# Attention sink as a column of the scores, weights normalised on ScalarE, and three steps moved in VectorE's order

## The reference, cut to what matters

```python
def swa_sink_attention(q, k, v, sinks):
    ...
    s = jnp.einsum("bnqhgd,bnkhd->bnhgqk", qb, kb, ...) * (HEAD_DIM ** -0.5)
    ...
    s = jnp.where(mask[None, :, None, None], s, NEG)
    sk = sinks.astype(jnp.float32).reshape(N_KV_HEADS, GROUP)[:, :, None, None]
    m = jnp.maximum(jnp.max(s, axis=-1, keepdims=True), sk)
    e = jnp.exp(s - m)
    p = e / (jnp.sum(e, axis=-1, keepdims=True) + jnp.exp(sk - m))
    o = jnp.einsum("bnhgqk,bnkhd->bnqhgd", p.astype(v.dtype), vb)
```

## Time and profile before

| what | value |
|---|---|
| median of 3 runs | 2660.0 us (2658.65 to 2663.03) |
| the profiled execution | 2658.19 us, of which the span 2656.4 us |
| TensorE matmuls busy | 2619.3 us (99%) |
| VectorE busy | 1601.4 us (60%) |
| ScalarE busy | 1028.5 us (39%) |
| GpSimd busy | 410.3 us (15%) |
| mean granted clock of TensorE | 0.998 of full speed |
| 762 to 854 us (first half of the beats) | TensorE 82.1, VectorE 84.1, ScalarE 58.1 of 92 us |
| 854 to 942 us (second half) | TensorE 87.8, VectorE 80.3, ScalarE 61.3 of 88 us |

### The profile page before, as it was taken

One profiled execution on the slowest core, in us unless ns is written; L12 is line 12 of the kernel. 1 busy time (PEld: TensorE's weight loads), 2 busy tenths in 40 slices (PEclk: granted clock), 3 DMA queues, 4 the chain that ended last, 5 costly groups with the idle time before them and its releaser, 6 DMA issues.

```text
span 2656.4 us, 33800 instructions
## 1 busy us (share of the span) xinstructions
PE 2619.3 (99%) x12616; PEld 2116.1 (80%) x12616; DVE 1601.4 (60%) x2440; ACT 1028.5 (39%) x1334; POOL 410.3 (15%) x147
## 2 busy tenths in 40 slices
PE   8999999999999999999999999999999999999998
PEld 6767888888876778888888888888888888888886
DVE  4467211213999976579998988888344444444444
ACT  4465322214346763232223455555332222222223
POOL 0001455542010003424444000000000000000000
PEclk9999999999999999999999999999999999999999
DMA  5111222222222222223333365465565555555552
GB/s 184 48 48 69 97 102 97 99 95 95 95 84 76 68 80 96 95 95 145 148 142 143 135 230 192 186 233 201 198 229 189 189 189 191 195 197 195 194 196 95
DMA packets 121737, 374.37 MB, mean 141 GB/s; under 512 B 7553, under 2 KB 73217, under 8 KB 92737
## 3 DMA queue, kind: packets, MB, share of 16 engines
q1 hardware_dynamic: 117968, 333.74, 35.5%
q10 hardware_dynamic: 2016, 35.26, 3.4%
q0 software_dynamic: 1680, 4.46, 0.6%
HBM read 301.86 MB, written 69.21 MB: 140 GB/s over the span
## 4 chain that ended last, share of the span: by engine, by line
PE 83%; DVE 13%; issue 2%; ACT 2%; DMA 0%; DVEq 0%; POOL 0%; POOLq 0%; ACTq 0%
PE ps L1042 26%; PE ps L1044 25%; PE ps L1043 25%; PE ps L1552 2%; DVE cand_t L2179 1%; DVE z L1910 1%; DVE cand_t L2175 1%; DVE sel L2181 1%; DVE wl L1640 1%; DVE topi L2141 1%; DVE topi L2151 1%; DVE sc L2144 1%; DVE sel L2184 1%; DVE bpos L2141 1%; DVE bpos L2151 1%
## 5 line engine op out<-in xcount | busy, mean ns | idle before, releaser
L1042 PE MATMUL ps<-hh,wh 128*128 128x512 f32 x1968 | 783.3, 398 | 9.3 <-DVE wl L1646 8.0
L1044 PE MATMUL ps<-hh,wl 128*128 128x512 f32 x1968 | 768.8, 391 | 0.0
L1043 PE MATMUL ps<-hl,wh 128*128 128x512 f32 x1968 | 767.8, 390 | 0.0
L531 ACT ACTIVATE wh<-raw 128x2048 fp32r<-128x2048 f32 x217 | 414.9, 1912 | 771.2 <-PE ps L1044 769.9
L2208 DVE TENSOR_TENSOR wl<-raw,wh 128x2048 fp32r<-128x2048 f32 x101 | 231.3, 2290 | 432.8 <-ACT wh L531 432.8
L1042 PEld LDWEIGHTS ps<-hh,wh 128*128 128x128 f32 x1968 | 370.2, 188 | 98.9 <-issue 15.6
L1044 PEld LDWEIGHTS ps<-hh,wl 128*128 128x128 f32 x1968 | 370.0, 188 | 79.3
L1043 PEld LDWEIGHTS ps<-hl,wh 128*128 128x128 f32 x1968 | 370.7, 188 | 74.3 <-issue 1.0
L1042 PE MATMUL ps<-gah,wh 128*128 128x512 f32 x1024 | 398.7, 389 | 0.0
L1044 PE MATMUL ps<-gah,wl 128*128 128x512 f32 x1024 | 398.7, 389 | 0.0
L1043 PE MATMUL ps<-gal,wh 128*128 128x512 f32 x1024 | 398.7, 389 | 0.0
(11 more groups left out here) (259 smaller groups left out, 3006.8 us busy)
## 6 DMA issues: line engine op xcount, KB each, us to landing
raw<-in_w_slots SPq DMA_DIRECT2D x217, 1024.0 KB, 4.8
a_spill<-ast SPq DMA_DIRECT2D x64, 512.0 KB, 2.6
gate_table<-stage ACTq DMA_DIRECT2D x8, 4096.0 KB, 13.0
at<-a_spill SPq DMA_DIRECT2D x64, 512.0 KB, 5.8
tt<-gate_table SPq DMA_DIRECT2D x64, 512.0 KB, 6.8
lnb<-z POOLq DMA_DIRECT2D x36, 64.0 KB, 1.9
xT<-in_x SPq DMA_DIRECT2D x4, 512.0 KB, 7.2
bt<-in_rel_tiles POOLq DMA_DIRECT2D x1, 2048.0 KB, 12.2
```

The lines of the kernel that those rows point to most:

```text
L531: act.activation(wh[:, b, :], raw[:, b, :], ACT.Copy).then_inc(sem("w_hi"), 1)
L1042: nc.tensor.matmul(bank, whi, xhi, start=start, stop=False)
L1043: nc.tensor.matmul(bank, whi, xlo, start=False, stop=False)
L1044: return nc.tensor.matmul(bank, wlo, xhi, start=False, stop=stop)
```

## The change

- The buffer `tmp` gets four more columns. Seen by the attention (`spr`), it is now two steps of two heads of 257 columns: the last is the sink's.
- GpSimd writes -sink into that column (`sink_column`), for every step, between the swaps in its queue. It waits until the Exp of two steps earlier is done.
- ScalarE's `exps` takes exp over the scores and the sink's column at once, so that the accumulated sum is already the denominator. The two activations for exp(sink - m) go.
- The reciprocal moves to ScalarE: Ln of the sum, then Exp of minus that, each waiting for the one before on its own engine. `scaled(n)` now follows `exps(n)` in the same beat.
- VectorE's `shares` goes. Its tap moves to the end of the beat.
- In VectorE's order the low part at t = 6 goes ahead of the five taps of that tile (those of t = 8, 10, ... stay behind theirs). The rotation of K2 goes from t = 20, behind taps and low part, to t = 19, ahead of the seven taps; that of Q2 stays at t = 21 but goes ahead of the taps.
- Behind the beats VectorE does 12 taps instead of 2 before the last `y_low`.

```diff
--- before.py
+++ after.py
@@ -210,7 +210,8 @@
         def esb(name, shape, dt=F32, stack=None):
             return (stack or early).enter_context(nc.sbuf_tensor(name, shape, dt))
 
-        tmp = esb("tmp", [P, 2, S])
+        tmp_all = esb("tmp_all", [P, 2 * S + 4])
+        tmp = tmp_all[:, 0:2 * S].rearrange("p (a n) -> p a n", a=2)
         sqb = esb("sqb", [P, 2, S])
         lnb = esb("lnb", [P, 2, S])
 
@@ -251,7 +252,8 @@
         nsink = esb("nsink", [P, 2 * SWA_PAIRS], stack=two)
         kdup = esb("kdup", [P, 2, S], stack=two)
 
-        spr, spt = (x.rearrange("p r (e n) -> p r e n", e=2) for x in (tmp[:, :, :], sqb[:, :, :]))
+        spr = tmp_all[:, :].rearrange("p (r e n) -> p r e n", r=2, e=2)
+        spt = sqb[:, :, :].rearrange("p r (e n) -> p r e n", e=2)
         swapped = lnb[:, 0, :]
 
         two.close()
@@ -497,9 +499,23 @@
                     of = to + HD // 2 if to % HD == 0 else to - HD // 2
                     pool.dma_start(swapped[to:to + HD // 2, :], u_tile(tile)[of:of + HD // 2, :]).then_inc(sem("swap_in"), 16)
 
+            def sink_column(n):
+
+                p = n // NT
+                if n == 0:
+                    pool.wait_ge(sem("rp_s"), 1)
+                if n >= 2:
+                    pool.wait_ge(sem("sw_e"), 2 * n - 2)
+                pool.tensor_copy(spr[:, n % 2, :, 2 * P:2 * P + 1],
+                                 nsink[:, 2 * p:2 * p + 2].rearrange("p (e n) -> p e n", n=1)).then_inc(sem("sw_k"), 1)
+
             swap_halves(K2, 0)
-            for p in range(SWA_PAIRS):
-                swap_halves(Q2 + p, p + 1)
+            swap_halves(Q2, 1)
+            swap_halves(Q2 + 1, 2)
+            for n in range(SWA_STEPS):
+                sink_column(n)
+                if n % NT == 2 and n // NT + 2 < SWA_PAIRS:
+                    swap_halves(Q2 + n // NT + 2, n // NT + 3)
 
             pool.wait_ge(sem("w_lo"), FIRST["co"] + 2 + 2)
             lows(FIRST["co"] + 2, FIRST["out2"] + 2)
@@ -783,19 +799,21 @@
 
                 c, st, p = swa_cols(n), sstat[:, n % 2, :], n // NT
                 act.wait_ge(sem("sw_m"), 2 * n + 2)
+                act.wait_ge(sem("sw_k"), n + 1)
                 for e in range(2):
-                    act.activation(spr[:, n % 2, e, c:], spr[:, n % 2, e, c:], ACT.Exp, bias=st[:, 2 + e:3 + e], scale=-1.0,
-                                   accum_out=st[:, 6 + e:7 + e]).then_inc(sem("sw_e"), 1)
-                for e in range(2):
-                    act.activation(st[:, 8 + e:9 + e], st[:, 2 + e:3 + e], ACT.Exp, bias=v("sinks", 2 * p + e)
-                                   ).then_inc(sem("sw_e"), 1)
+                    act.activation(spr[:, n % 2, e, c:2 * P + 1], spr[:, n % 2, e, c:2 * P + 1], ACT.Exp,
+                                   bias=st[:, 2 + e:3 + e], scale=-1.0, accum_out=st[:, 6 + e:7 + e]).then_inc(sem("sw_e"), 1)
 
             def scaled(n):
 
                 c, st = swa_cols(n), sstat[:, n % 2, :]
+                act.wait_ge(sem("sw_e"), 2 * n + 2)
+                act.activation(st[:, 8:10], st[:, 6:8], ACT.Ln).then_inc(sem("sw_a"), 1)
+                act.wait_ge(sem("sw_a"), n + 1)
+                act.activation(st[:, 12:14], st[:, 8:10], ACT.Exp, scale=-1.0).then_inc(sem("sw_r"), 1)
                 act.wait_ge(sem("sw_r"), n + 1)
                 for e in range(2):
-                    act.activation(spr[:, n % 2, e, c:], spr[:, n % 2, e, c:], ACT.Copy, scale=st[:, 12 + e:13 + e]
+                    act.activation(spr[:, n % 2, e, c:2 * P], spr[:, n % 2, e, c:2 * P], ACT.Copy, scale=st[:, 12 + e:13 + e]
                                    ).then_inc(sem("sw_p"), 1)
 
             def turned_weights(n):
@@ -822,12 +840,11 @@
             def beat(n):
                 if n >= 7 and (n - 7) % NT == 0:
                     heads_out((n - 7) // NT)
-                if 0 <= n - 1 < SWA_STEPS:
-                    scaled(n - 1)
                 if 0 <= n - 2 < SWA_STEPS:
                     turned_weights(n - 2)
                 if n < SWA_STEPS:
                     exps(n)
+                    scaled(n)
 
             def in2_out(t):
 
@@ -1968,20 +1985,11 @@
                 if n >= 2:
                     dve.wait_ge(sem("sw_t"), n - 1)
                 for e in range(2):
-                    dve.tensor_tensor_reduce(spr[:, n % 2, e, c:], ps[:, 3 + e, c:2 * P], msk[:, c:], -SCALE,
+                    dve.tensor_tensor_reduce(spr[:, n % 2, e, c:2 * P], ps[:, 3 + e, c:2 * P], msk[:, c:], -SCALE,
                                              nsink[:, 2 * p + e:2 * p + e + 1], ALU.add, ALU.min,
                                              accum_out=st[:, 2 + e:3 + e]).then_inc(sem("sw_m"), 1)
                 taps(1)
 
-            def shares(n):
-
-                st = sstat[:, n % 2, :]
-                dve.wait_ge(sem("sw_e"), 4 * n + 4)
-                dve.tensor_tensor(st[:, 10:12], st[:, 6:8], st[:, 8:10], ALU.add).then_inc(sem("sw_a"), 1)
-                taps(1)
-                dve.wait_ge(sem("sw_a"), n + 1)
-                dve.reciprocal(st[:, 12:14], st[:, 10:12]).then_inc(sem("sw_r"), 1)
-
             def y_low(p):
 
                 dve.wait_ge(sem("at_h"), p + 1)
@@ -1989,15 +1997,13 @@
 
             def beat(n):
                 taps(1)
-                if 0 <= n - 1 < SWA_STEPS:
-                    shares(n - 1)
                 if n < SWA_STEPS:
                     masked(n)
                 if n % NT == 1 and n // NT + 1 < SWA_PAIRS:
                     roped(Q2 + n // NT + 1, n // NT + 2, "sw_q")
                 if n >= 9 and (n - 9) % NT == 0:
                     y_low((n - 9) // NT)
-                taps(1)
+                taps(2)
 
             g0 = FIRST["in2"]
             dve.wait_ge(sem("ns"), 1)
@@ -2009,16 +2015,18 @@
                     beat(n)
                 if t <= RAW_TILES:
                     scaled_out(t - 1)
-                if RAW_TILES <= t < BEAT_TILE0:
-                    taps(7 if t % 2 else 5)
-                if t % 2 == 0 and t < Z2_TILES:
+                if t % 2 == 0 and t <= RAW_TILES:
                     weight_low(g0 + t // 2 + 1)
                 if t == 4:
                     scaled_x()
-                if ORDER2[t - 1] == Q2 + 1:
+                if ORDER2[t - 1] == Q2:
                     roped(K2, 0, "rk")
                 if ORDER2[t - 1] == Q2 + 2:
                     roped(Q2, 1, "sw_q")
+                if RAW_TILES <= t < BEAT_TILE0:
+                    taps(7 if t % 2 else 5)
+                if t % 2 == 0 and RAW_TILES < t < Z2_TILES:
+                    weight_low(g0 + t // 2 + 1)
                 if t == 30:
                     ln_sums(0)
                     ln_sums(1)
@@ -2034,7 +2042,7 @@
                 dve.tensor_tensor(u_tile(GATTN + n), u_tile(GATTN + n), ps[:, AO_BANKS[n], :], ALU.mult
                                   ).then_inc(sem("ev_ao"), 1)
 
-            taps(2)
+            taps(12)
             y_low(SWA_PAIRS - 1)
             weight_low(g0 + 1)
             taps(KD * conv_steps)
```

## The result

The changed kernel takes 2683.2 us (median of 6 runs, 2682.3 to 2683.7) beside 2659.9 us for the kernel before on the same chip (6 runs, 2658.3 to 2663.0): ratio 1.0088, 95% interval 1.0078 to 1.0097. That is outside the range that I gave, on the other side of no change.

The account below looks back on a forecast made before the run. TensorE's queue, busy 2619.3 of 2656.4 us, was taken as the bound. Opening +1.1, later waits -6.2, half speed -1.9 and +1.0 gave -6.0: 2652.2 for the profiled execution, 2654.0 us as median, range 2649.5 to 2660.

Parts of the forecast that it names:

- The rest: Outside the main terms: one more column in two Exps under 0.01 us; the 16-byte longer buffer shifting others, nothing.
- the likeliest case: The forecast itself, 2654.0 us for the whole kernel, given chance 0.48 and a range between 2651.5 and 2657.
- my two signs of being wrong: Attention stage: step-2 masking ending before 777 us, or taps beside the column copies lasting longer than 0.75 us.
- The rival for the slower side: Ln and Exp each load a table in every beat, or shifted buffers cost something: 2686 us, chance 0.07.
- The chain from Ln to the scaling: ScalarE, each beat: dependent Ln and Exp cost 0.65 us, 0.2 more than the removed activations, 6 us in all.
- The opening (+1.1): Attention's start: moved low part and rotations leave VectorE idle 2.1 us, and TensorE passes step 2's masking 1.1 us later.
- The next low parts have more room than that: Opening, VectorE: running 2.1 us later does no harm; the low part at 752.71 serves a tile nine microseconds later.
- Half speed in the opening (+1.0): Near 775 us: a 3.5 us TensorE wait brings a 1.9 us half-speed stretch, half vanishing in the next ScalarE wait.
- The waits behind it (-6.2): After the opening: TensorE's waits for maskings, ScalarE's copies and layer-norm sums fall from 8.5 to 2.3 us.
- the end (-1.9): Attention's tail: the half-speed stretch at 961.87, behind the 2.85 us wait at 961.22, disappears, saving 1.9 us.
- 64 steps of 0.08 us: VectorE's shares: removing thirty-two pairs of small operations, each stepping by 0.08 us, frees 4.9 us of its time.
- GpSimd's copies: Attention beats: sink-column copies and VectorE taps exclude each other, adding 3.2 to 12.8 us on VectorE; 2655.3 to 2659.1, chance 0.17.

Follow-up runs that it names:

- e5_still: Kernel after, with the four extra columns overlapping a buffer idle in the attention stage, so nothing behind moves: 2652.1 us, 0.997 of the kernel before.
- e2_shift: Kernel before with only an unused 32-byte buffer per partition ahead of the shared buffer `tmp`, shifting all behind it by 32 bytes: 2689.2 us, ratio 1.0107.
- e6_low_back: e5_still with the low part of tile 6 put back behind its five taps, rotations still ahead: 2651.1 us beside 2652.1.
- s1_sweep: Kernel before with only the gather's streamed buffers padded to distances of 128, 192, 256 and 512 bytes from the weights', modulo 2048: 2673.5 us, one run.
- e8_best: e5_still with three of tile 6's taps ahead of the low part, two taps instead of seven before the first masking, five moved to later beats: 2648.0 us, 0.9954.

## Why the prediction was wrong, by its own steps

**The rest: "I know no cost, and matmuls last 0.39 whether they stream from one buffer or another, so nothing".** This is the step that failed. I had seen that the buffer grows by 16 bytes and moves all behind it. My reason for pricing that at nothing was a row of durations in a layout in which all these buffers lay a multiple of 2048 bytes from the weights: it could not show what another distance does, and a duration rounded to 0.01 us hides 6.7 ns. The term is +31.0 us (after against e5_still), +29.5 alone (e2_shift). Without it the forecast would have been near: e5_still is 7.8 us under before, where the sum said 6.0, inside the likeliest case's range. Neither of my two signs of being wrong came up (the step-2 masking ends at 779 us in e5_still, the taps stay at 0.73 us): both watched only the stage that was changed.

**The rival for the slower side** named "any cost of the shifted buffers" but priced a table load. That its 2686 us lie near the measured 2683.2 is luck, for no table load comes in the beats (the first behind 764 us is one of 1.28 us at 949.51, behind them). Ln and Exp, on ScalarE in the kernel after:

```profile
777.01 0.20 ACT L811 ACTIVATE sstat<-sstat 128x2 f32<-128x2 f32 x1
777.25 0.20 ACT L813 ACTIVATE sstat<-sstat 128x2 f32<-128x2 f32 x1
777.48 0.91 ACT L816 ACTIVATE tmp_all<-tmp_all,sstat 128x256 f32<-128x256 f32 x2
```

The chain from Ln to the scaling is 0.47 us, not 0.65: equal to the two activations that went. I had taken the duration of the activations of one column with a bias per partition (L790), 284 ns; these, of two columns and without one, last 204 (mean of 32 each), and start 0.24 us apart.

**The opening (+1.1).** In e5_still the first low part starts at 682.60, VectorE idle for 2.00 us ahead, as described. The next starts at 695.50, and TensorE waits for it:

```profile
682.60 2.29 DVE L1658 TENSOR_TENSOR wl<-raw,wh 128x2048 fp32r<-128x2048 f32 x1 [2.00 <-ACT wh L548]
...
695.50 2.28 DVE L1658 TENSOR_TENSOR wl<-raw,wh 128x2048 fp32r<-128x2048 f32 x1
```

```profile
697.83 0.50 PE L1060 MATMUL ps<-hh,wh 128*128 128x512 f32 x1 [1.71 <-DVE wl L1658]
```

In the kernel before, that low part is the second of these:

```profile
682.74 2.29 DVE L1640 TENSOR_TENSOR wl<-raw,wh 128x2048 fp32r<-128x2048 f32 x1
...
692.84 2.29 DVE L1640 TENSOR_TENSOR wl<-raw,wh 128x2048 fp32r<-128x2048 f32 x1
```

The masking of step 2 releases TensorE at 779.35 (forecast 779.0). Its waits are 0.63, 1.71, 0.65 and 3.31, 6.3 us, where before had 5.8; the forecast had 0.6, none, 0.5, 2.4 and 3.5. I missed that the next low part would be late: "The next low parts have more room than that" looked only at the one at 752.71, and the 1.71 us at 698 are for the very next. Where TensorE has lost them, it no longer waits at its first beat. By e6_low_back the early low part is no gain.

**Half speed in the opening (+1.0).** Right in kind, too small in the profiled execution. In e5_still, behind the 3.31 us of idle TensorE:

```profile
779.35 1.22 PE L1339 MATMUL ps<-kdup,z 64*128 64x256 f32 x4 [3.31 <-DVE sstat L1989]
780.50 1.12 PE L1350 MATMUL ps<-cst,lt 128*128 128x128 f32 x4
```

The four score matmuls end after 1.15 us of steps, against 0.64 in the kernel after, where the clock fell only later. From 779.35 to the first matmul of the next piece it takes 2.82 us instead of the 1.59 before, the step behind 0.60 instead of 0.34 and the six after it 2.56 instead of 1.39: 2.7 us in all. I had let half of it vanish in ScalarE's next wait, and that is still 1.31 (1.47 before). My reason, that 3.5 us of waiting is longer than waits that did no harm, is not borne out: in other executions waits of 1.50 to 2.57 us were followed by half speed too (last section).

**The waits behind it (-6.2) and the end (-1.9).** 8.5 us down to 1.8 us (1.31 and 0.52, both for ScalarE's copies): -6.7. The wait at 961.22 and its half speed are gone. Both steps hold. The balance in rows is +0.5 +2.7 -6.7 -1.9 = -5.4. Set beside before's, matmul by matmul, e5_still gains 5.1 us in the stage; 0.6 us were lost in the first 60 us of the kernel, long before the stage, so that the spans give -4.6. The medians give -7.8 with an interval of 4.8 to 11.2: e5_still's profiled execution is the slowest of its six (2653.7), and before's (2658.2) lies 1.7 us under the median. So the sum of -6.0 is near in part by luck, as the opening was put too dear by 0.6 and the half speed too cheap by 1.7.

One figure of the working is off by itself: 64 steps of 0.08 us are 5.1 us and not 4.9. The sum does not use it.

**GpSimd's copies.** Refuted as a cost, by the doubled copies. They do stretch, from 0.18 to 3.09 us in e5_still, but beside them VectorE's low parts keep their 2.29 us and its taps their 0.73: only GpSimd pays here.

## What to carry to other kernels

An edit that lengthens a buffer moves what is allocated behind it; here 16 bytes more made 4528 matmuls that stream from there 5.9 to 6.7 ns slower each. Where a phase that no line of the diff touches gets slower at full clock and without waits, compare the steps of its matmuls to the nanosecond and then the addresses; an unused pad of the same size in the old kernel tests it in one run. Here layouts with the streamed buffers a multiple of 256 bytes from the weights' were free (226.7 ns; 256 itself by one kernel alone), and the extra columns fitted into a neighbour that was idle. In a full queue, move filler work to where that queue waits, and look whether it waits there for something that the move doesn't bring.

## What I had not expected of the hardware

- The gather's float32 matmuls of 512 columns step by 226.7 ns in the kernel before and in e5_still and by 233.3 in the kernel after and e2_shift, by the distance in SBUF between their streamed operand and their weights: 31 us of 2683. Moving both together changed nothing (2659.2 beside 2659.7). Why, and why the distance of 64 bytes (228.9) lies between, no run here shows.
- A GpSimd copy of two elements per partition took between 0.18 and 3.09 us in e5_still; 31 of the 32 ran beside VectorE, whose low parts kept their 2.29 us, and the one with nothing beside it (914.94) took 0.19.
- How long TensorE waited does not by itself tell whether half speed follows. The waits of 2.60 and 1.85 us in the kernel before left the clock at full speed (1.00 from 764 to 790 us); in s1_sweep, whose attention code and buffers are the same, those of 2.57, 1.87 and 1.53 us were each followed by half speed (clock 0.80 from 764 to 790, 0.97 from 790 to 850), and so were 2.57, 1.85 and 1.50 in e2_shift. That of 3.31 us in e5_still was followed by it at once, that of 3.33 in the kernel after 1.7 us later (784.02 to 785.72), that of 1.73 in e8_best not at all. The wait at TensorE's first beat in s1_sweep, to be set beside the one at 764.60 in the earlier trace rows:

```profile
764.90 0.80 PE L1328 MATMUL ps<-kdup,z 64*128 64x128 f32 x4 [2.57 <-DVE z L1967]
765.63 0.79 PE L1049 MATMUL ps<-hh,wh 128*128 128x512 f32 x1
766.22 0.63 PE L1050 MATMUL ps<-hl,wh 128*128 128x512 f32 x1
766.65 0.63 PE L1051 MATMUL ps<-hh,wl 128*128 128x512 f32 x1
```
